# A two-block transformer kernel: splits, transposes and norms of the recurrent layer's end, the last layer's entry and its last heads put in another order

## What is computed

```python
def rglru_mixer(...):      # recurrent layer, 16 blocks of 128 features
    u, g = split(h @ w_in); xc = dwconv(u)
    r, i = sigmoid(xc @ gate_w + gate_b)
    a = exp(-8 * r * softplus(-lam)); b = sqrt(1 - a*a) * (i * xc)
    h_t = a_t * h_(t-1) + b_t                  # both directions
    y = ((h_fwd + h_bwd) * silu(g)) @ w_out
def diff_attn_mixer(...):  # last layer, 16 heads, context output not needed
    q, k, v, g = split(h @ w_in)               # q, k normalized per head, rotated
    attn = softmax(q1 k1) - lam * softmax(q2 k2)
    o = rms_norm(attn @ v, subln_g) * (1 - lam_init)
    y = (o * silu(g)) @ w_out
x = x + gate * y
```

## Time and profile before

| what | value |
|---|---|
| median of 3 runs | 2595.79 us (2592.61 to 2597.37) |
| profiled execution, its own time | 2592.13 us |
| span of its profile | 2590.3 us |
| PE busy | 2509.2 us, 97% of the span |
| weight load (PEld) busy | 1958.0 us, 76% |
| DVE busy | 1444.5 us, 56% |
| ACT busy | 1178.6 us, 46% |
| POOL busy | 259.2 us, 10% |
| mean granted TensorE clock | 0.99 |

### The profile page before, as it was taken

One profiled execution on the slowest core, in us unless ns is written; L12 is line 12 of the kernel. 1 busy time (PEld: TensorE's weight loads), 2 busy tenths in 40 slices (PEclk: granted clock), 3 DMA queues, 4 the chain that ended last, 5 costly groups with the idle time before them and its releaser, 6 DMA issues.

```text
span 2590.3 us, 31456 instructions
## 1 busy us (share of the span) xinstructions
PE 2509.2 (97%) x12080; PEld 1958.0 (76%) x12080; DVE 1444.5 (56%) x1905; ACT 1178.6 (46%) x1727; POOL 259.2 (10%) x138
## 2 busy tenths in 40 slices
PE   6999999999999999999999999899899999999978
PEld 5887777777777667788777777787787877878767
DVE  4644444544545455566767676635545474654764
ACT  6444334553444434456565655424425344253542
POOL 0000000000000000002555554001200000000000
PEclk9999999999999999999999999999999999999999
DMA  6568777736787888865333333324334243342323
GB/s 218 179 187 271 239 240 249 245 106 217 240 278 265 268 288 280 282 230 147 98 93 97 93 93 92 107 82 146 114 98 136 84 122 98 97 130 85 123 86 130
DMA packets 277298, 429.42 MB, mean 166 GB/s; under 512 B 14502, under 2 KB 93116, under 8 KB 276028
## 3 DMA queue, kind: packets, MB, share of 16 engines
q1 hardware_dynamic: 275772, 422.28, 51.4%
q10 hardware_dynamic: 1408, 5.51, 0.6%
HBM read 425.64 MB, written 2.10 MB: 165 GB/s over the span
## 4 chain that ended last, share of the span: by engine, by line
PE 89%; DVE 4%; ACT 4%; issue 1%; DMA 1%; SPq 0%; ACTq 0%; DVEq 0%
PE ps L725 62%; PE ps L1106 13%; PE ps L798 4%; PE ps L1089 2%; ACT ring_hi L1332 1%; PE ps L876 1%; PE ps L903 1%; PE ps L1212 1%; PE ps L1230 1%; PE ps L776 1%; PE ps L1061 1%; DVE ring_lo L1794 1%; PE ps L809 1%; PE ps L888 1%; ACT second_block L1689 0%
## 5 line engine op out<-in xcount | busy, mean ns | idle before, releaser
L1332 ACT CAST ring_hi<-ring 128x1024 fp32r<-128x1024 f32 (+2 forms) x598 | 619.6, 1039 | 1044.5 <-PE ps L725 598.7
L1794 DVE TENSOR_TENSOR ring_lo<-ring,ring_hi 128x1024 fp32r<-128x1024 f32 (+2 forms) x522 | 629.2, 1212 | 793.9 <-ACT ring_hi L1332 791.4
L725 PE MATMUL ps<-ring_hi,act_hi 128*128 128x512 f32 (+2 forms) x1272 | 513.6, 404 | 9.9 <-issue 4.4
L725 PE MATMUL ps<-ring_hi,act_lo 128*128 128x512 f32 (+2 forms) x1272 | 493.4, 388 | 0.0
L725 PE MATMUL ps<-ring_lo,act_hi 128*128 128x512 f32 (+2 forms) x1272 | 491.6, 386 | 0.0
L725 PE MATMUL ps<-ring_hi,features_hi 128*128 128x512 f32 x1152 | 462.4, 401 | 15.1 <-DVE features_lo L2230 7.4
L725 PE MATMUL ps<-ring_hi,features_lo 128*128 128x512 f32 x1152 | 452.5, 393 | 0.0
L725 PE MATMUL ps<-ring_lo,features_hi 128*128 128x512 f32 x1152 | 452.3, 393 | 0.0
L725 PEld LDWEIGHTS ps<-ring_hi,act_hi 128*128 128x128 f32 x1272 | 240.3, 189 | 112.2 <-issue 47.2
L725 PEld LDWEIGHTS ps<-ring_hi,features_hi 128*128 128x128 f32 x1152 | 218.8, 190 | 84.7 <-issue 27.2
L725 PEld LDWEIGHTS ps<-ring_hi,act_lo 128*128 128x128 f32 x1272 | 239.9, 189 | 51.1
(11 more groups left out here) (246 smaller groups left out, 2417.7 us busy)
## 6 DMA issues: line engine op xcount, KB each, us to landing
ring<-in_mod_w SPq DMA_DIRECT2D x192, 512.0 KB, 5.1
ring<-in_att_w_in SPq DMA_DIRECT2D x128, 512.0 KB, 3.7
ring<-in_ev_w_in SPq DMA_DIRECT2D x104, 512.0 KB, 4.8
ring<-in_od_w_in SPq DMA_DIRECT2D x96, 512.0 KB, 5.5
ring<-in_lru_w_in SPq DMA_DIRECT2D x64, 512.0 KB, 4.1
ring<-in_ev_w_out SPq DMA_DIRECT2D x40, 512.0 KB, 4.8
ring<-in_lru_w_out SPq DMA_DIRECT2D x40, 512.0 KB, 3.7
ring<-in_od_w_out SPq DMA_DIRECT2D x36, 512.0 KB, 4.5
```

What stands on the lines that cost most here:

```text
L725: mm = pe.matmul(PS[:, bank, 0:n], a, w[:, k - k0, :], start=(k == k_first and j == 0), stop=(k == k_last and j == 2))
L1332: act.copy(high(U, n), raw(U, n)).then_inc(s_hi, 1)
L1794: dve.tensor_tensor(out=low(U, n), in0=raw(U, n), in1=high(U, n).bitcast(F32), op=ALU.subtract).then_inc(s_lo, 1)
```

## The change

```diff
@@ shared_lo
-    return u % 2 == 1 and (name == "lru_out" and u >= 32 or name == "att_in" and u < 16)
+    return name == "lru_out" and u < 4 or u % 2 == 1 and (name == "lru_out" and u >= 32 or name == "att_in" and u < 16)
@@
-LAT_BEHIND = {2: (0, 1), 3: (2,), 4: (3, 4), 5: (5,), 6: (6,), 7: (7,)}
+LAT_BEHIND = {2: (), 3: (0, 1), 4: (2, 3), 5: (4,), 6: (5, 6), 7: (7,)}
+ROWS_IN_KEYS = {5: (0, 1), 6: (2, 3), 7: (4, 5), 8: (6,), 9: (7,)}
@@
-        OUT_FILL = ((0, 1), (2,), (3, 4), (5,), (6, 7), (8,), (9, 10), (11,))
+        OUT_FILL = ((0,), (1, 2), (3,), (4, 5), (6,), (7, 8), (9,), (10, 11))
@@ sync: the last store (chunk 3)
+                    for tt in range(TT):
+                        sp.wait_ge(s_re, RES0["att_out"] + 4 + tt)
+                        sp.dma_start(ov[:, tt, cols], X[:, tt, cols]).then_inc(s_out, 16)
@@ tensor: entry of the last layer
-                if u == 4:
+                for j in ROWS_IN_KEYS.get(u, ()):
                     pe.wait_ge(s_xn, 5)
-                if u >= 4:
-                    to_features(tiles_of(CN), 2 * (u - 4), 2)
-            features_ready()
+                    to_features(tiles_of(CN), j, 1)
             for u in range(8, 16):
+                pe.wait_ge(s_xl, lat + 8 + (u - 8) + 1)
                 att_unit(-1, u)
+                for j in ROWS_IN_KEYS.get(u, ()):
+                    to_features(tiles_of(CN), j, 1)
@@ tensor: last heads
                 if s < 7:
                     scores(last, s + 1)
-                for j in OUT_FILL[s]:
+                if s:
+                    weights_values(last, s - 1)
+                for n, j in enumerate(OUT_FILL[s]):
                     if j == OUT_AHEAD:
                         pe.wait_ge(s_dqe, 4 * GROUPS)
-                    if j == OUT_FILL[s][-1] and len(OUT_FILL[s]) > 1:
+                    out_unit(j)
+                    if n == 0:
                         weights_transposes(last, s)
-                    out_unit(j)
-                if len(OUT_FILL[s]) == 1:
-                    weights_transposes(last, s)
-                weights_values(last, s)
+            weights_values(last, 7)
             for j in range(8, 12):
                 gate_row(j, 4 + j % 2, j - 1 if j >= 10 else 0)
             pe.wait_ge(s_oe, 8 * GROUPS)
-            y_transposes(last, 6)
+            for q in range(2):
+                pe.wait_ge(s_oy, GROUPS + q)
...
+                mm.then_inc(s_dyt, 1)
@@ scalar: end of the recurrent layer
+                if ahead is None:
+                    act.wait_ge(s_wused, UNIT0["lru_out"])
+                    y_hi(0, 4, FTH, YL)
                 act.wait_ge(s_gt, n(1))
                 act.wait_ge(s_y, n(2))
...
-                if ahead is None:
-                    y_hi(0, 4, FTH, YL)
@@ scalar: entry of the last layer (vector the same way, with split_features)
+            att_hi(-1, range(5, 10))
+            for u, behind in ROWS_IN_KEYS.items():
+                if u == 7:
+                    take_chunk(-1, 0, RQK[:, 4:6, :], 2, 2)
+                for j in behind:
+                    scale_features(mod_scale(3), mod_shift(1, 1), TMP_B, j, 1)
+                att_hi(-1, [5 + u])
+            att_hi(-1, range(15, 20))
@@ scalar: last heads
+            def output_squares(s):
+                act.wait_ge(s_oe, last * 8 + s + 1)
+                g = s % 2 * 4 + s // 2
+                act.activation(BUF[:, 1920:2048], OS[:, s % 2, s // 2 * P:(s // 2 + 1) * P], ACT.Square, accum_out=DS8[:, g:g + 1]).then_inc(s_osq, 1)
             for s in range(8):
                 if s < 7:
                     exponentials(last, s + 1)
+                if s:
+                    output_squares(s - 1)
+                his("att_out", [OUT_FILL[s][0] + 4])
                 weights_out(last, s)
+                his("att_out", [j + 4 for j in OUT_FILL[s][1:]])
+            output_squares(7)
+            act.wait_ge(s_osq, 8)
+            outputs_root(last)
+            for j in range(8, 12):
                 gate_rows_out(G_ATT, j, 4 + j % 2)
+            for q in range(2):
+                k = 2 * OUT_AHEAD + 2 * q
+                act.wait_ge(s_dyt, GROUPS + q)
+                act.copy(DYH[:, k:k + 2, :], PS[:, 6 + q, :].rearrange("p (k s) -> p k s", k=2)).then_inc(s_yhi, 2)
@@ vector: end of the recurrent layer
-            los("lru_out", range(0, 4))
             y_lo(0, 4, FTH, FTL, YL, 0)
@@ vector: last heads
                 combine(last, s, link)
                 if s < 7:
                     maxima(last, s + 1)
+                if s:
+                    output(last, s - 1)
                 los("att_out", [j + 4 for j in OUT_FILL[s]])
-                output(last, s)
-                if s == 2:
+                if s == 1:
+                    dve.wait_ge(s_dqe, 4 * GROUPS)
+                    tail_link(dve.tensor_tensor(out=RG[:].rearrange("p t (j c) -> p (t j) c", c=P), in0=RG[:].rearrange("p t (j c) -> p (t j) c", c=P),
+                                                in1=SUBG.unsqueeze(1).to_broadcast([P, 8, P]), op=ALU.mult))
                     dve.wait_ge(s_e2, 4 * GROUPS)
-                if s in (2, 3):
-                    gate_diagonals(8 + s - 2, 1, 0)
-            outputs_square(last, link)
+                if s in (3, 4):
+                    gate_diagonals(8 + s - 3, 1, 0)
+            output(last, 7)
+            dve.wait_ge(s_osq, 8)
+            dve.tensor_scalar(DS8, DS8, 1.0 / P, EPS, ALU.mult, ALU.add).then_inc(s_om, 1)
+            dve.wait_ge(s_or, GROUPS)
+            tail_link(dve.reciprocal(DS8, DS8))
+            for q in range(2):
+                for j in range(2 * q, 2 * q + 2):
+                    for tt in range(TT):
+                        o, g = OS[:, tt, j * P:(j + 1) * P], tt * 4 + j
+                        ins = dve.scalar_tensor_tensor(out=o, in0=o, scalar=DS8[:, g:g + 1], in1=RG[:, tt, j * P:(j + 1) * P],
+                                                       op0=ALU.mult, op1=ALU.mult)
+                ins.then_inc(s_oy, 1)
             for j in range(10, 12):
                 gate_diagonals(j, 1, 0)
-            outputs_gate(last, link)
-            y_lo(2 * OUT_AHEAD, KT - 2 * OUT_AHEAD, DYH, DYL, DYT, KT)
+            for q in range(2):
+                k = 2 * OUT_AHEAD + 2 * q
+                dve.wait_ge(s_yhi, KT + k + 2)
+                dve.tensor_tensor(out=DYL[:, k:k + 2, :], in0=PS[:, 6 + q, :].rearrange("p (k s) -> p k s", k=2),
+                                  in1=DYH[:, k:k + 2, :].bitcast(F32), op=ALU.subtract).then_inc(s_ylo, 2)
...
-            att_residual(3)
+            def last_residual(tt):
+
+                if tt == 0:
+                    dve.wait_ge(s_gd, len(EVICTED) + 1)
...
+            last_residual(0)
+            last_residual(1)
@@ gpsimd
             lru_ix(KT - 2)
+            for u in range(4):
+                weights_lo(UNIT0["lru_out"] + u)
             lru_ix(KT - 1)
```

More of the change, by code:

```diff
@@ L2443, in projections_behind @@
                         y_lo(8 + 2 * j, 2, DYH, DYL, DYT, KT)
-            att_lo(-1, range(5, 8))
-            for j in range(4):
-                att_lo(-1, [8 + j])
-                split_features(part(FTH, 0), part(FTL, 0), TMP_B, 2 * j, 2)
-            att_lo(-1, range(12, 20))
+            att_lo(-1, range(5, 10))
+            for u, behind in ROWS_IN_KEYS.items():
+                for j in behind:
+                    split_features(part(FTH, 0), part(FTL, 0), TMP_B, j, 1)
+                att_lo(-1, [5 + u])
+            att_lo(-1, range(15, 20))
             projections_behind(-1, False)
@@ L2466, in _ @@
             link, done = linker(s_dstep, last, PER_HEADS)
+            tail_link, _ = linker(s_tstep, last, PER_TAIL)
             for s in range(8):
```

37 lines of the change are left out of this document (16 added, 21 removed).

## The result

The changed kernel takes 2578.74 us (median of five runs, 2577.60 to 2581.66); the kernel before, measured beside it, 2592.61 us (2590.03 to 2597.37). The ratio is 0.9943, 95% interval [0.9929, 0.9958]: 14 us faster, where I had said 10.2. A second series of the same kernel gave 2580.66 against 2594.35 us, 0.9949 [0.9937, 0.9961]. My 2585.5 us lies 6.8 us over the first median: 3.2 us of that are the base (I scaled to a median of 2595.79 us of three runs; beside the changed kernel it was 2592.61), 3.6 us are the change itself.

The account below looks back on a forecast made before the run. PE, busy 97% of the span, bounds the kernel; only its standstills and slow clock can be saved. +3.0 - 12.2 + 1.4 - 0.5 - 1.9 = -10.2 us, on the median's scale 2585.5 us; 8-in-10 range 2578 to 2592.

Parts of the forecast that it names:

- A: End of the recurrent layer: four lo splits on POOL, y_hi before the last sigmoids; PE starts the product later, +3.0 us.
- B and C: Latent transposes a unit later, context rows transposed in the keys: PE's waits go and clock is regained, -12.2 us.
- D: Last heads with weights_values behind the next scores, +1.4 us; the stretch behind the last values to the next unit, -0.5 us.
- my laying: PE, ACT and DVE laid out over the last heads' eight steps: PE waits 8.6 us in old order, 10.0 in new.
- So the wait of 7.0 is not saved: Last heads: weights_values' five waits for ACT's copy, 7.0 us, stay, being late for DVE's maxima.
- rival 2: Last heads do gain: the 7.0 us of waits go, D is -7.5 instead of +0.9, total 2577.1 us; chance 0.13.
- the table load of 1.28 us: Behind the last heads, before the root: ACT's table load taken as exposed at 1.28 us; 1.4 us longer by the skill page.
- E: The end: first tile's residual beside the second tile's matmuls, -1.3 us, and last store halved, about -0.6; together -1.9 us.
- the price of the lower clock: Clock lost behind PE's waits at the context rows' transposes and keys: 0.9 and 1.6 us, together 2.5 us.
- which end, at half clock as before, near 11: Behind the last heads: the last gate rows end near 11 us, within 13.5 us to the next unit.
- rival 4: Slower: the last heads' loop of scores, exponentials, combine and maxima costs over 1.9 us more per step; 2602 us, chance 0.03.

Follow-up runs that it names:

- experiment 2: Kernel before, with only the output product's four lo splits on POOL and y_hi ahead of the last sigmoids; 2595.55 us, ratio 1.0009.
- experiment 6: Changed kernel with the four lo splits back on DVE, the early y_hi kept; 2576.64 us, ratio 0.9931 to the kernel before.
- experiment 12: Kernel of experiment 6 with the first two of the four lo splits on POOL; 2576.71 us, ratio 0.9931 to the kernel before.
- experiments 9 and 11: On experiment 6: 9 puts last two gate diagonals before DVE's root wait, 2570.38 us; 11 adds DVE operations moved to last step and ACT's copy first, 2566.31 us.
- experiment 3: Kernel before, with only the new last heads, the tail behind them, and the last residual and store in halves; 2590.70 us, ratio 0.9986.

## Why the prediction was right in sign and too small in size

**A, +3.0: right.** The pair of traces has +3.0 (7.95 against 4.98 us of wait), experiment 2 measured +2.4, experiment 6 gets back 4.0 against 3.9 in the trace. The step "The change gives block 14 the same four splits, so I take 25.2 us" held (1604.57 to 1629.82, 25.25 us), and so did the sequence load, sigmoids, PE. What I did not see is that the price is not one per split (experiment 12).

**B and C, -12.2: right in kind, too small by 1.2.** From the product's start to the first scores it is 809.28, 807.93, 809.65 and 808.00 us in four traces without the part and 795.17 to 795.58 in ten with it: -13.4. The three waits, 9.6 us of standing, went whole and nothing came in their place; I had -9.7. The term that was too small is the clock: I had 2.5 us for it and it is 3.8, what is left of the 13.4. I counted six matmuls at the lower clock and a state of 3.1 us, which no row gave; in the profile of before the matmuls stayed slow to about 1863.5, five us behind the first. Behind the transposes at 1839.72, for which I had counted 0.9 us, four more matmuls were slow, about 0.8 us. Nor is it a constant: the same transposes behind the same wait of 2.46 us took 1.93 us in one trace and 1.09 in three others.

**D, +1.4 and -0.5: right in kind.** The heads cost 0.7 us and the tail gives 0.3 (13.3 against 13.65 us on average). The order of waits was as laid out, with `scores` at 2.0 us, the copy at step 6 at 3.0 (3.7 in my laying). In the laying PE waits 8.6 and 10.0 us, in the traces it stands 7.8 and 8.4: the laying was too long for both orders, by more for the new one. "So the wait of 7.0 is not saved" is what the traces show, and rival 2 is out. The pair of traces alone would have said +3.9, a miss of mine that isn't one. On the table load of 1.28 us, taken as exposed in full, the tail bears me out: the row of the root is at 2511.07, 0.01 us after its end, and a drain of 1.4 us more isn't there.

**The step that failed** is the price of the lower clock. At the entry the sum had 2.5 us for it where 3.8 were measured, and behind the heads it had nothing: I priced that clock at the context rows and nowhere else. "which end, at half clock as before, near 11" was said of the gate rows, and I didn't follow that clock into the next units. There, the old tail costs 57.0 us for 240 matmuls on average of five traces (56.35 to 57.46), and the new one 54.7 in each of nine: **-2.3 us**. In the old tail the last wait before these units is 2.4 us and the first matmul takes 0.79 us; in the new one it is 0.8 to 1.1 and 0.50. That it is this last wait that keeps the clock down is likely but not shown by itself, since the waits ahead of it changed too (3.0 and up to 1.7 us before, one of 5.5 after). The 5.5 us are not what gives the 54.7, since experiments 9 and 11 have 2.7 us in their place and 54.7 us as well.

**E, -1.9: nearly.** -1.5. From the last matmul's end to the last addition's it is 1.65 us against 2.7, so 1.0 of the 1.3 us came; and the last store, half as large, ends the span 2.7 us later instead of 3.2, so 0.5 of the 0.6. No run has this part alone; it is 4.3 us in all ten traces with the new end and 5.8 in all four with the old one.

With the averages the sum is 3.0 - 13.4 + 0.7 - 0.3 - 2.3 - 1.5 = -13.8 us, and the two series measured -14.8 and -13.2 by their ratios; the parts of D and E in it, 0.7 - 0.3 - 2.3 - 1.5 = -3.4, agree with the -3.6 of experiment 3. Of the 3.6 us that were missing, 2.3 are behind the heads, 1.2 at the entry, where the clock was, and 0.7 in the heads, less 0.2 in the tail and 0.4 at the end. That the pair of traces gave about my -10.2 was luck: its +3.9 for the heads and its offset of 1.15 hid the two terms of the clock. The other 3.2 us of the 6.8 are the base: the kernel before had medians of 2592.61, 2593.11, 2594.35 and 2595.68 us in four series, so a median of three runs carries an error of its own of 1 to 3 us, and a ratio would have been the better thing to forecast. (The 2602 of rival 4 is 2601 by its own terms, 2595.8 + 5.2.)

## What to carry to other kernels

Price a wait of PE at its length and at what the clock loses behind it, and follow that loss into the next stage until a row is back at full rate; behind the heads the last wait ahead of the dense stretch became 1.3 to 1.6 us shorter, and the stretch took 2.3 us less on top of that. Before a difference of two traces of 3 us is explained by the order of work, look at the standing (span less busy) and at the granted clock of the stretch apart: here the first was the same to 0.1 us in all five traces of the old order, and what the second cost differed by up to 4.5 us between them. A split that is moved to the idle engine is free only as long as the delay that it gives VectorE stays inside the next wait's slack, and an engine that idles for a table load is a place for work that is in the way elsewhere.

## What was unexpected in the hardware

Nearly the whole scatter of this kernel goes with TensorE's clock. In the 51 runs of the kernel before beside the experiments, taken by the mean granted clock of each run, the span averages 2595.5 us at 0.988 (nine runs), 2591.9 at 0.990 (24), 2588.1 at 0.992 (six) and 2586.2 at 0.993 (two). In the heads PE's standing is the same in each trace of one order to 0.1 us (old) or 0.8 us (new), and what differs between those traces is behind which of the waits of 2 to 3 us the clock falls to 1.2 GHz, and for how long. That it falls behind some and not behind others of the same length, in the same kernel, was not explained by these runs.
